# Up projection of a feed-forward block by Strassen's algorithm, squared ReLU as one VectorE operation

## The reference

```
h   = x @ w_in                      # 2048 x 5124, then RG-LRU and two attentions
x   = LN1(alpha * x + concat(rms(y_A), rms(y_B), rms(y_C)) @ w_out)     # 2048 x 2048
hdn = square(relu(x @ w_up))                                            # 2048 x 8192
x   = LN2(alpha * x + hdn @ w_down)                                     # 8192 x 2048
```

## Time and profile before

| | |
|---|---|
| median of 3 runs | 2600.16 us (2599.29 to 2600.46) |
| profiled execution: its own time / its span | 2600.43 us / 2598.6 us |
| mean granted TensorE clock | 0.986 |
| PE / DVE / ACT / POOL busy | 97% / 37% / 28% / 8% |
| instructions of PE (matmuls) | 18,465 |
| moved by DMA | 243.00 MB, mean 94 GB/s |

### The profile page before, as it was taken

The page is one execution under the profiler, slowest core; times in us unless marked ns, Lnnn a source line. Parts: engine busy times, 40 slices in busy tenths (PEclk is TensorE's granted clock), DMA queues, the critical chain, the costliest instruction groups (busy, mean ns, idle before and its releaser), DMA issues.

```text
span 2598.6 us, 43706 instructions
## 1 busy us (share of the span) xinstructions
PE 2515.6 (97%) x18465; PEld 2470.1 (95%) x18465; DVE 972.0 (37%) x1004; ACT 735.2 (28%) x842; POOL 216.5 (8%) x231
## 2 busy tenths in 40 slices
PE   8999999988997989999999999999999999999997
PEld 7999999977886979999999999999999999999997
DVE  3312555244455373323323322322332322332258
ACT  3222444233343153222213213212212212312332
POOL 2000333000110266000000000000000000000000
PEclk9999999989998989999999999999999999999999
DMA  7222333343341212222222322222222222232344
GB/s 211 72 81 83 107 95 101 108 138 107 114 136 35 84 60 81 81 81 81 82 85 75 95 82 81 81 81 81 81 81 81 81 83 83 77 95 71 93 158 158
DMA packets 235482, 243.00 MB, mean 94 GB/s; under 512 B 8596, under 2 KB 224856, under 8 KB 234856
## 3 DMA queue, kind: packets, MB, share of 16 engines
q1 hardware_dynamic: 217424, 221.69, 27.5%
q10 hardware_dynamic: 16200, 12.89, 1.5%
q0 software_dynamic: 1808, 7.72, 0.9%
HBM read 225.70 MB, written 18.16 MB: 94 GB/s over the span
## 4 chain that ended last, share of the span: by engine, by line
PE 94%; DVE 3%; ACT 1%; issue 1%; DMA 0%; ACTq 0%; DVEq 0%; SPq 0%; POOL 0%; POOLq 0%
PE psum L384 85%; PE psum L1548 4%; DVE x_lo L1013 1%; PE psum L1448 1%; PE psum L1362 1%; PE psum L1403 0%; DVE resid L914 0%; PE psum L1417 0%; ACT w_hi L370 0%; PE psum L1535 0%; DMA raw<-in_w_in 0%; PE psum L1435 0%; DVE rms L986 0%; PE psum L1399 0%; PE psum L1450 0%
## 5 line engine op out<-in xcount | busy, mean ns | idle before, releaser
L384 PE MATMUL psum<-x_hi,w_hi 128*128 128x288 f32 (+1 forms) x3328 | 721.4, 298 | 10.4 <-DVE x_lo L1013 3.7
L384 PE MATMUL psum<-x_hi,w_lo 128*128 128x288 f32 (+1 forms) x3328 | 717.5, 297 | 0.0
L384 PE MATMUL psum<-x_lo,w_hi 128*128 128x288 f32 (+1 forms) x3328 | 717.1, 297 | 0.0
L374 DVE TENSOR_TENSOR w_lo<-raw,w_hi 128x2048 fp32r<-128x2048 f32 x192 | 449.9, 2343 | 681.3 <-ACT w_hi L370 681.3
L370 ACT ACTIVATE w_hi<-raw 128x2048 fp32r<-128x2048 f32 x192 | 367.5, 1914 | 1166.0 <-PE psum L384 1098.1
L384 PEld LDWEIGHTS psum<-x_hi,w_hi 128*128 128x128 f32 x3328 | 539.5, 190 | 15.8 <-DVE x_lo L1013 5.6
L384 PEld LDWEIGHTS psum<-x_hi,w_lo 128*128 128x128 f32 x3328 | 539.2, 190 | 0.0
L384 PEld LDWEIGHTS psum<-x_lo,w_hi 128*128 128x128 f32 x3328 | 538.5, 189 | 0.0
L384 PE MATMUL psum<-h_lo,w_hi 128*128 128x288 f32 x1792 | 384.2, 295 | 0.0
L384 PE MATMUL psum<-h_hi,w_lo 128*128 128x288 f32 x1792 | 381.0, 293 | 0.0
L384 PE MATMUL psum<-h_hi,w_hi 128*128 128x288 f32 x1792 | 379.9, 293 | 0.7 <-DVE acc L996 0.7
(11 more groups left out here) (272 smaller groups left out, 1833.5 us busy)
## 6 DMA issues: line engine op xcount, KB each, us to landing
raw<-in_w_down SPq DMA_DIRECT2D x72, 1024.0 KB, 5.4
raw<-in_w_up SPq DMA_DIRECT2D x64, 1024.0 KB, 5.7
raw<-in_w_in SPq DMA_DIRECT2D x40, 1024.0 KB, 5.3
raw<-in_w_out SPq DMA_DIRECT2D x16, 1024.0 KB, 5.5
qkv_scratch<-stage ACTq DMA_DIRECT2D x24, 288.0 KB, 2.1
x_rows<-in_x_prompt SPq DMA_DIRECT2D x16, 256.0 KB, 7.8
q<-qkv_scratch SPq DMA_DIRECT2D x8, 288.0 KB, 2.9
k<-qkv_scratch SPq DMA_DIRECT2D x8, 288.0 KB, 3.2
```

The lines of the kernel that those rows point to most:

```text
L374: dve.tensor_tensor(WL[s][:, :, :], RAW[s][:, :, :], WH[s][:, :, :].bitcast(F32), ALU.subtract).then_inc(lo_done, 1)
L384: last_mm = pe.matmul(PS[:, 2 * to + h, 0:c], w, x[:, kk, HALF * h:HALF * h + c], start=(first and n == 0), stop=(final and n == 2))
```

## The change

The up projection is done over 16 super blocks of 512 hidden columns. In each, the weights are four tiles (A00, A01, A10, A11: first index the half of the hidden columns, second the half of the rows) and the normalised x has four quarters (b00, b01, b10, b11: half of the width, half of the tokens). Strassen's algorithm in Winograd's form needs seven tile products of 48 matmuls where the plain way has eight.

The first two products (A00 with F1 = b00, A01 with F2 = b10) are done for all 16 super blocks in a first stage ("1A"): `snapshot` copies the first product to memory (V), and the sum of both, C00, is rectified, squared and stored. The other five products per super block follow in a second stage ("1B"), with sums of weight tiles formed by VectorE (`sigma1` to `sigma4`) and sums of x quarters (F3 to F7) formed once, during 1A. All four weight tiles are loaded again in 1B. Results are rectified and squared by one `scalar_tensor_tensor` each (`relu_square`: min or max with 0, times the value itself) and stored to memory; `load_h` brings a chunk of h back for the down projection, where ScalarE and VectorE split it.

The layer norm is done in full before the up projection (gain, shift and 1/deviation applied to x), for the first 288 tokens during the second half of the output projection, which now takes its 8 tiles twice, once for each half of the tokens, and for the other 288 during 1A. POOL stores x1 to memory, and `acc` is loaded from there. The instructions of the output projection's first half, the down projection's matmuls and the last stage stay.

The core of the diff, in the order SP, ACT, DVE, PE. `hi_1a`, `hi_1b` and `lo_1b` are `hi` and `lo` with other sources; `factor_hi` and `factor_lo` split a quarter of x (2304 columns), `shifted` applies gain and shift in four operations of 288 columns, `scaled` multiplies 1152 columns by 1/deviation.

```diff
+            for v in range(2, 16):
+                load(sp, N_O2 + v + 1, v % 2, w_view["out"][:, UK:2 * UK, UC * (v % 8):UC * (v % 8) + UC])
+            with sp.Fori(0, 14) as g:
+                load_group(sp, g + G_1A, [up_unit(0, s, g) for s in range(2)])
+            sp.wait_ge(combo, 4)
+            sp.wait_ge(f_lo, 6)
+            sp.dma_start(S10[0][:, :, :], up_unit(1, 0, 0)).then_inc(a10_in, 16)
+            sp.dma_start(S11[0][:, :, :], up_unit(1, 1, 0)).then_inc(a11_in, 16)
...
+            sp.wait_ge(lo_done, N_1B + 1)
+            sp.dma_start(A00[:, :, :], up_unit(0, 0, 0)).then_inc(a00_in, 16)
+            sp.wait_ge(lo_done, N_1B + 2)
+            sp.dma_start(S11[1][:, :, :], up_unit(0, 1, 0)).then_inc(a01_in, 16)
...
+            def load_1b(it, q):
+                g = it * 2 + q
+                sp.wait_ge(sig, g * 4 + 3)
+                sp.dma_start(A00[:, :, :], up_unit(0, 0, g + 1)).then_inc(a00_in, 16)
+                sp.wait_ge(lo_done, unit_1b(g, 1) + 3)
+                sp.dma_start(S10[1 - q][:, :, :], up_unit(1, 0, g + 1)).then_inc(a10_in, 16)
+                sp.wait_ge(sig, g * 4 + 4)
+                sp.dma_start(S11[1 - q][:, :, :], up_unit(1, 1, g + 1)).then_inc(a11_in, 16)
+                sp.wait_ge(v_out[1 - q], it * 16 + 16)
+                sp.dma_start(VV[1 - q][:, :, :], v_rows(g + 1)).then_inc(v_in[1 - q], 16)
+                sp.wait_ge(lo_done, unit_1b(g, 4) + 3)
+                sp.dma_start(S11[q][:, :, :], up_unit(0, 1, g + 1)).then_inc(a01_in, 16)
...
+                    squares(v - 9, 0)
+                elif v == 12:
+                    deviation(0)
+                elif v == 13:
+                    shifted(0, 0)
+                    shifted(1, 0)
+                    act.wait_ge(x1_done, UK)
+                    factor_hi(F1, X1["b00"])
+                elif v == 14:
+                    shifted(2, 0)
+                    shifted(3, 0)
+                    act.wait_ge(x1_done, KT)
+                    factor_hi(F2, X1["b10"])
...
+            for g in range(N_SB):
+                it, q = divmod(g, 2)
+                if g:
+                    finish_c00((g - 1) // 2, (g - 1) % 2)
+                if g == 5:
+                    deviation(1)
+                elif g == 8:
+                    act.wait_ge(combo, 1)
+                    factor_hi(F5, X1["b00"])
+                elif g == 9:
+                    factor_hi(F3, X1["b11"])
+                elif g == 12:
+                    act.wait_ge(combo, 4)
+                    act.wait_ge(f_lo, 5)
+                    factor_hi(F4, X1["b10"])
+                snapshot(it, q)
+                if g + 1 < N_SB:
+                    hi_1a(N_1A + 2 * g + 2)
                 else:
...
+            def hi_1b(n, par, src, sigma):
+                act.wait_ge(sig, sigma)
+                act.wait_ge(unit_done, n + 1)
+                act.activation(WH[par][:, :, :], src[:, :, :], ACT.Copy).then_inc(hi_done, 1)
+            def superblock(it, q, end=False):
+                g = it * 2 + q
+                hi_1b(unit_1b(g, 2), q, S10[q], g * 4 + 3)
+                hi_1b(unit_1b(g, 3), 1 - q, SIG2, g * 4 + 4)
+                hi_1b(unit_1b(g, 4), q, S11[q], g * 4 + 1)
+                act.wait_ge(post, g * 9 + 14)
+                act.dma_start(h_rows(1, g)[:, :, HALF:TOK], CQ[1][:, :, :]).then_inc(c_out[1], 16)
+                if not end:
+                    hi_1b(unit_1b(g, 5), 1 - q, SIG2, g * 4 + 6)
...
+            for v in range(16):
+                for m in range(2):
+                    add_out(v, m)
...
+                elif v == 13:
+                    rstd(0)
+                    scaled(0, 0)
+                n = N_O2 + v + 2
+                lo(dve, n // 2, n % 2)
...
+                elif v == 13:
+                    scaled(1, 0)
+                elif v == 14:
+                    scaled(2, 0)
+                    scaled(3, 0)
+                    factor_lo(F1, X1["b00"], 1)
+                elif v == 15:
+                    factor_lo(F2, X1["b10"], 2)
+            for a in range(2 * N_SB):
+                n = N_1A + a + 2
+                g = a // 2
+                if a % 2:
+                    dve.wait_ge(unit_done, N_1A + a + 3)
+                    dve.wait_ge(snap, a + 1)
+                    dve.wait_ge(ca_out[g % 2], g // 2 * 16 + 16)
+                    dve.tensor_tensor(CQ[g % 2][:, :, :], PS[:, 2:4, 0:HALF], VV[g % 2][:, :, :], ALU.add).then_inc(c00_add, 1)
+                if a < 2 * N_SB - 2:
+                    lo(dve, n // 2, n % 2)
+                if a in (0, 1):
...
+                elif a == 10:
+                    rstd(1)
+                    scaled(0, 1)
+                    scaled(1, 1)
+                elif a == 11:
+                    scaled(2, 1)
+                    scaled(3, 1)
+                elif a == 15:
+                    dve.wait_ge(x1_done, 2 * KT)
+                    dve.wait_ge(xs_out, 32)
+                    dve.tensor_tensor(X1["b00"], X1["b00"], X1["b01"], ALU.subtract).then_inc(combo, 1)
+                    dve.wait_ge(combo, 1)
...
+                elif a == 17:
+                    factor_lo(F5, X1["b00"], 3)
...
+            def sigma1(g, q):
+                dve.wait_ge(a10_in, g * 16 + 16)
+                dve.wait_ge(a11_in, g * 16 + 16)
+                dve.tensor_tensor(S10[1 - q][:, :, :], S10[q][:, :, :], S11[q][:, :, :], ALU.add).then_inc(sig, 1)
+                dve.wait_ge(sig, g * 4 + 1)
+            def sigma2(g, q):
+                dve.wait_ge(a00_in, g * 16 + 16)
+                dve.tensor_tensor(SIG2[:, :, :], S10[1 - q][:, :, :], A00[:, :, :], ALU.add).then_inc(sig, 1)
+            def sigma3(g, q):
+                dve.tensor_tensor(S10[q][:, :, :], S10[q][:, :, :], A00[:, :, :], ALU.add).then_inc(sig, 1)
+            def sigma4(g, q):
+                dve.wait_ge(lo_done, unit_1b(g, 0) + 3)
+                dve.wait_ge(a01_in, g * 16 + 16)
+                dve.tensor_tensor(SIG2[:, :, :], SIG2[:, :, :], S11[1 - q][:, :, :], ALU.add).then_inc(sig, 1)
+            def relu_square(T, side):
+                t = T[:, :, :]
+                dve.scalar_tensor_tensor(t, t, 0.0, t, side, ALU.mult).then_inc(post, 1)
...
+            def superblock(it, q, end=False):
+                g = it * 2 + q
+                dve.wait_ge(unit_done, unit_1b(g, 0) + 3)
+                dve.wait_ge(v_in[q], it * 16 + 16)
+                dve.tensor_tensor(VV[q][:, :, :], PS[:, 0:2, 0:HALF], VV[q][:, :, :], ALU.add).then_inc(post, 1)
+                sigma4(g, q)
+                lo_1b(unit_1b(g, 2), q, S10[q])
+                dve.wait_ge(unit_done, unit_1b(g, 1) + 3)
+                dve.wait_ge(post, g * 9 + 10)
+                dve.wait_ge(c_out[0], g * 16 + 16)
+                dve.tensor_tensor(CQ[0][:, :, :], PS[:, 2:4, 0:HALF], VV[q][:, :, :], ALU.add).then_inc(post, 1)
+                dve.wait_ge(sig, g * 4 + 4)
+                lo_1b(unit_1b(g, 3), 1 - q, SIG2)
+                if not end:
+                    dve.wait_ge(lo_done, unit_1b(g, 2) + 3)
+                    sigma1(g + 1, 1 - q)
+                dve.wait_ge(unit_done, unit_1b(g, 2) + 3)
+                dve.wait_ge(post, g * 9 + 11)
+                dve.wait_ge(c_out[1], g * 16 + 16)
+                dve.tensor_tensor(CQ[1][:, :, :], PS[:, 4:6, 0:HALF], CQ[0][:, :, :], ALU.add).then_inc(post, 1)
+                dve.tensor_tensor(VV[q][:, :, :], PS[:, 4:6, 0:HALF], VV[q][:, :, :], ALU.add).then_inc(post, 1)
+                dve.wait_ge(post, g * 9 + 12)
+                relu_square(CQ[1], ALU.min)
+                if not end:
+                    dve.wait_ge(lo_done, unit_1b(g, 3) + 3)
+                    sigma2(g + 1, 1 - q)
+                lo_1b(unit_1b(g, 4), q, S11[q])
+                dve.wait_ge(unit_done, unit_1b(g, 3) + 3)
+                dve.tensor_tensor(CQ[0][:, :, :], PS[:, 6:8, 0:HALF], CQ[0][:, :, :], ALU.add).then_inc(post, 1)
+                dve.wait_ge(post, g * 9 + 15)
+                relu_square(CQ[0], ALU.max)
+                if not end:
...
+                dve.wait_ge(unit_done, unit_1b(g, 4) + 3)
+                dve.wait_ge(post, g * 9 + 13)
+                dve.tensor_tensor(VV[q][:, :, :], PS[:, 2:4, 0:HALF], VV[q][:, :, :], ALU.add).then_inc(post, 1)
+                dve.wait_ge(post, g * 9 + 17)
+                relu_square(VV[q], ALU.min)
+                if not end:
+                    sigma3(g + 1, 1 - q)
+                    lo_1b(unit_1b(g, 6), q, S10[q])
...
+            dve.wait_ge(unit_done, N_1B + 1)
+            sigma1(0, 0)
+            sigma2(0, 0)
+            dve.wait_ge(sig, 2)
+            lo_1b(N_1B, 0, SIG2)
+            sigma3(0, 0)
+            lo_1b(N_1B + 1, 1, S10[1])
...
+            def superblock(it, q):
+                g = it * 2 + q
+                for j, (F, bank, before) in enumerate(((F6, 0, 1), (F5, 2, 8), (F7, 4, 4), (F3, 6, 6), (F4, 2, 11))):
+                    pe.wait_ge(lo_done, unit_1b(g, j) + 3)
```

(84 more changed lines are left out.)

630 lines of the change are left out of this document (357 added, 273 removed).

## The result

The changed kernel takes 2553.57 us, median of 4 runs (2552.57 to 2555.91), where the kernel before took 2600.14 beside it: a ratio of 0.9823, interval 0.9806 to 0.984. It is 46.6 us faster. The forecast was 2529, with a range up to 2562. The kernel before, timed anew beside each group of experiments, took 2599.6, 2599.6 and 2600.3, so a gain is sure to about half a microsecond at best.

What follows compares the result with a forecast made beforehand. The prediction took PE's matmuls, 133.4 ns each, to bound the kernel. Savings of 102.4, 19.8 and 1.1 us less added costs gave -71.5 from 2600.43: 2529 us, own range 2512 to 2540, stated range 2508 to 2562.

Steps and rivals of the forecast that it cites:

- (e): From output projection to first product: PE idle 8.3 us, plus 2.8 for a clock restart, 11.1 us in all.
- (f): Waits within the first two products' 32 units, where ScalarE's other work delays weight splits: 11.2 us in all, no restart counted.
- (g): Seam from first to second product stage: PE idle 9.8 us, plus 2.8 for a restart, 12.6 us.
- (i): From the last product to the down projection: PE waits 5.7 us, plus 2.8 for a restart, 8.5 us.
- rival 1: VectorE sets the second stage's pace, by a slower relu_square or handover losses: 13.5 to 30 us more, about 2549; chance 0.18.
- rival 2: Second-stage weights land late, as A00, A10 and A11 are issued within 5.5 us: 22 us more, 2551; chance 0.10.
- (h): Second stage's 16 super blocks, where VectorE's order decides: 0.4 us late for each of 15, 6.0 us.
- (d): Seven ones products, at 0.24 us each: 1.7 us.
- the 0.7 us for VectorE: Down stage: allowance of 0.7 us for the added copies, subtractions and a load, with VectorE busy under a third.
- its 2.8: One cold clock restart of PE after idling, priced at 2.8 us.
- Rival 3: The clock falls once in every super block, at 2.8 us each: 45 us more, 2573; chance 0.04.
- Rival 4: Loads bind in both product stages, making the kernel slower: 83 us more at 160 GB/s; chance 0.03.

Runs made afterwards that it cites:

- experiment 5: Changed kernel with A00 of the next super block loaded last of the three (A10, A11, A00) in the second stage: 2547.87 us.
- experiment 7: Changed kernel with the output projection's first unit doing three products for each half of the columns behind each row of y: 2549.38 us.
- experiments 8 and 10: TensorE's down-stage loop written out straight for the last six chunks: in 8 against the changed kernel, 2555.66 us; in 10 added to experiment 9, 2504.08 us.
- experiment 2: Changed kernel with rectify and square as two VectorE operations in place of one in the second stage: 2568.64 us.
- experiment 4: Changed kernel with ScalarE's order altered, splits of weights before shifts and factor splits, in output projection and first stage: 2532.66 us.
- experiment 3: Changed kernel with sigma1 and sigma2 of the first super block formed beside the first stage's last unit, not after it: 2544.40 us.
- experiment 9: Changed kernel with the edits of experiment 3, experiment 4, experiment 5 and experiment 7, and the third quarter's relu_square behind the fifth unit's low part: 2507.36 us.
- experiment 8: Changed kernel with TensorE's program of the down stage written out straight for its last six chunks, without the loop: 2555.66 us.

## Why the prediction came out as it did

The method held: the records fell by 762, with 768 products gone and three ones products added, and the steps worked out as a walk along one chain hit their places: (e) 8.4 us idle for 8.3, (f) the waits before unit 13, F5, F7, F6 and F4 (4.2, 2.7, 2.1, 1.3, 1.8 us for 3.5, 1.7, 2.5, 1.2, 1.7; none at F3 for 0.6), (g) 9.8 for 9.8, (i) 5.7 for 5.7. The time was 24.7 us over the forecast, and nearly all of that lies in terms that were too small. The sum's own range, 2512 to 2540, missed it; the stated one held it by the room kept for rivals 1 and 2 (2549 and 2551). Their place was the second stage, which gave only 10.5 us of the 24.7, so that the time came out so near theirs is in good part luck. The terms:

- **(h), 10.5 us.** I put 0.4 us on each block and gave the loads nothing, with rival 2 (the loads land late) at 0.10. The 15 gaps sum to 16.8 us, for 6.0, and two things add up in them. By experiment 5 the late landing of A11 was worth 5.7 us: about rival 2's mechanism, a quarter of its price. I had compared the landing with the time that a load takes alone (5.4 us), and with a burst rate for three; with A00 and A10 ahead of it, A11 took 8. The other half is VectorE's chain, 0.77 us with the load out of the way (experiment 5), not 0.4 (and the chain as I wrote it down gave 0.3). "From unit 1 6.5, in time" was 6.7: hi 1.92, lo 2.21, sigma1 2.28 and 0.28 of semaphores, from the end of unit 1 (1442.25) to the addition behind sigma1 (1448.94) in the run of experiment 5. So rival 1 was as near as rival 2, by its second half: more was lost at the handovers, while relu_square cost what was forecast. That VectorE's work as a sum sets the pace falls: with the same work in another order no wait is left.
- **(f), 4.5 us.** The waits are 0.8 us over, nearly all the rest is the clock. "None is long enough to count a restart" was wrong: it fell behind the wait of 4.2 us, at 2.6 us of loss, and behind that of 2.1 (the section on the hardware has the rows).
- **(d), 1.7 us.** I misread: the x4 there are records, and one ones product leaves two of them. So four records are two products, one product takes 0.48 us and not 0.24, and the seven take 3.4: 0.7 too little in the output projection, 1.0 in the first stage.
- **The start of the output projection, 3.1 us**, in no term (0.3 of it are a wait before the variance product). I let the stage take as long as before, as matmuls stay in number. But the kernel before had 6 products to do behind each row of y that VectorE released, and the changed one 3: its first half was over before it could start the second. Experiment 7 gives 4.0 us back, more than the order had cost, by the shorter stretch at half rate.
- **Upstream, 3.4 us.** The first ones product stands at 797.44, for 794.01 before; in all ten experiments it lies between 796.27 and 797.77, so it belongs to the changed program. The input projection shows part of it, at an equal clock; the stretch from 60 to 230 us, first before, then after:

```profile
60.00:230.00 170.00, 170.00 (x1277) 169.03 (x1276) 41.88 (x35) 36.18 (x47) 0.86 (x6) 1.00 0.26 81
```
```profile
60.00:230.00 170.00, 170.00 (x1270) 169.02 (x1269) 42.75 (x35) 36.18 (x47) 0.86 (x6) 1.00 0.27 82
```

  Seven matmuls fewer in 170 us, 133.9 ns for 133.1, where the change touched nothing. All ten experiments show the same, 6 to 8 matmuls fewer than before. Why stays open; no experiment went there.
- **The down stage, 1.9 us.** The two pauses at the jumps back of TensorE's loop, 3.1 us in the chain of waits above, which I didn't count (experiments 8 and 10), while the 0.7 us for VectorE wasn't needed and the restart took some 0.9 less than its 2.8. 0.4 us stay unplaced.

With 0.2 us in the last stage the terms come to 25.3, for 25.4 by which the span is over the forecast's.

**Rival 3** (the clock falls in every block) is out: in the 510 us from 1180 the granted clock was 1.00, with a wait of about a microsecond each 33 us, and in the same stretch with two waits a block (experiment 2) it rounds to 1.00 again, with one fall in 30 waits, behind the longest of them, 2.0 us (the rows are below). Against the rule of the Trainium skill quoted there ("TensorE: Matmul & The Clock Gate", "A second HAM failure mode: psum-queue depth-cycling"), short idling between groups did not make the clock switch back and forth here; single longer pauses made it fall. **Rival 4** (the loads bind) is out too: the first stage moved 216 GB/s at a share of 0.70 and one load of it stands in the chain of waits (9.1 us, from 1036.46, on the way to the wait of 2.7 us), as a part of that wait at most.

## What to carry to other kernels

Price a load by how long it takes with the loads that are under way beside it, and issue loads in the order in which they are wanted. Where an engine is as busy as VectorE in the second stage (79% of it), its order can decide, and not its sum: walk every chain from one product to the next, the first too, and move what nobody waits for (a rectified result, a factor for later) behind what TensorE waits for. Where a unit is made smaller or reordered, ask also what stands behind each operand at its start, when these still trickle in.

## What the runs showed of the hardware

The clock behind a pause is not a matter of its length alone. TensorE's first matmul behind some pauses (in brackets the idle time) and the windows that begin with it: in the changed kernel at 1022.82, 1060.00 and 1068.68, in experiment 4 at 926.58, in experiment 2 at 1502.51 and in experiment 7 at 1112.53.

```profile
1022.82 0.61 PE L1841 MATMUL psum<-x_b_hi,w_hi 128*128 128x288 f32 x1 [4.21 <-DVE w_lo L409]
1060.00 0.40 PE L1841 MATMUL psum<-x_b_hi,w_hi 128*128 128x288 f32 x1 [2.66 <-DVE w_lo L409]
1068.68 0.40 PE L1841 MATMUL psum<-x_b_hi,w_hi 128*128 128x288 f32 x1 [2.08 <-DVE w_lo L409]
```
```profile
1022.80:1032.00 9.20, 9.19 (x50) 9.19 (x51) 4.80 (x4) 6.24 (x10) 1.17 (x1) 0.69 0.87 259
1060.00:1066.50 6.50, 6.50 (x48) 6.37 (x48) 3.26 (x3) 4.13 (x3) 0.00 (x0) 1.00 0.52 161
1068.60:1089.50 20.90, 20.82 (x145) 20.82 (x146) 16.14 (x9) 10.00 (x10) 0.00 (x0) 0.92 0.67 206
```
```profile
926.50:935.50 9.00, 8.92 (x56) 8.95 (x57) 5.05 (x3) 5.73 (x9) 1.28 (x1) 0.81 0.56 173
```
```profile
1502.51 0.53 PE L1843 MATMUL psum<-x_e,w_hi 128*128 128x288 f32 x2 [2.01 <-DVE w_lo L1348]
```
```profile
1502.50:1508.90 6.40, 6.39 (x36) 6.40 (x37) 3.97 (x4) 0.00 (x0) 0.00 (x0) 0.73 0.71 210
```
```profile
1112.53 0.39 PE L1841 MATMUL psum<-x_b_hi,w_hi 128*128 128x288 f32 x1 [1.80 <-DVE w_lo L409]
```
```profile
1112.50:1118.90 6.40, 6.37 (x36) 6.37 (x37) 5.24 (x3) 2.03 (x4) 0.00 (x0) 0.73 1.04 350
```

4.2 us: 0.69 over the next 9.2. 2.7 us: none. 2.1 us, one unit behind it: 0.92 over the next 21, with a first matmul at full speed, so the fall came a little later. 3.5 us: 0.81. And 3.1 us: 1.00 in experiment 3, 0.56 in experiment 9.

Nor is about 3 us an edge, for shorter pauses, with no other of over a microsecond in the 20 us before them, were followed by a fall as well: 2.0 us in experiment 2 (0.73 over the next 6.4), 2.45 us in experiment 8 (0.73), 1.8 us in experiment 7 (0.73). Of the ten pauses of 1.8 us in the first stages of all these traces two were followed by a fall, both in experiment 7. From 920 to 2500 us, in all twelve traces, no pause of 0.9 to 1.76 us was followed by one and every pause from 3.2 us on was; between them it went either way. So a restart has to be carried in the range for any pause of 1.8 to 3.2 us, not set to 0 or 2.8. Its price varied too: 48 matmuls took 2.6 us more behind the pause of 4.2 us, 1.6 more behind those of 2.0 and 2.45.

A reduction over the middle axis of 2304 columns took VectorE 4.45 us, where an elementwise operation of that size takes 2.55.
